# Strassen's seven products for both projections of a hybrid decoder layer

## The reference, cut to what matters

```python
h = rms_norm(x, norm_in)                      # x: 2048 x 1024
proj = h @ w_in                               # 1024 x 6400
cb, cc, cu, gate_c, q, k, v, gate_a = split(proj)   # k, v: 128 columns, the others 1024
conv_y = cb * short_conv(cc * cu, conv_w)     # causal, width 3
conv_y = rms_norm(conv_y, norm_conv_out) * silu(gate_c)
attn_y = sliding_window_attention(q, k, v, sinks)   # window 128, 16 heads, 2 kv heads
attn_y = rms_norm(attn_y, norm_attn_out) * silu(gate_a)
x = x + concat([conv_y, attn_y]) @ w_out      # 2048 x 1024
return rms_norm(x, norm_final)
```

## Time and profile before

| | |
|---|---|
| median of 3 runs | 1689.29 us (1688.45 to 1691.91) |
| span of the profiled execution | 1689.7 us |
| TensorE busy | 1638.5 us (97%) |
| VectorE busy | 1038.0 us (61%) |
| ScalarE busy | 560.3 us (33%) |
| GpSimd busy | 267.0 us (16%) |
| mean granted TensorE clock | 0.989 of full speed |

### The profile page before, as it was taken

How to read it: one execution, slowest core, us unless ns; L and a number is a source line. 1 busy time by engine, 2 the same in 40 slices (tenths; PEclk the granted TensorE clock), 3 DMA queues, 4 the chain that set the end, 5 groups by cost and what they waited for, 6 DMA issues and landing times.

```text
span 1689.7 us, 23074 instructions
## 1 busy us (share of the span) xinstructions
PE 1638.5 (97%) x7824; PEld 1370.7 (81%) x7824; DVE 1038.0 (61%) x2262; ACT 560.3 (33%) x1275; POOL 267.0 (16%) x229
## 2 busy tenths in 40 slices
PE   5999999999999998999999999999999899999996
PEld 4888888888888886788888888888888688888885
DVE  6376767667576758567667676766667643333332
ACT  6333433343333354333333333333333421111110
POOL 1021212122121302112122121312122000000000
PEclk9999999999999999999999999999999899999998
DMA  4112021121202152211121212112021532222220
GB/s 172 54 38 74 31 81 53 47 75 35 78 31 68 43 194 69 81 51 63 43 68 37 74 31 82 50 50 74 31 94 63 199 138 100 99 99 97 98 77 27
DMA packets 61774, 125.42 MB, mean 74 GB/s; under 512 B 4640, under 2 KB 37408, under 8 KB 59680
## 3 DMA queue, kind: packets, MB, share of 16 engines
q1 hardware_dynamic: 59424, 116.44, 20.2%
q0 software_dynamic: 2304, 8.39, 1.2%
HBM read 99.64 MB, written 25.17 MB: 74 GB/s over the span
## 4 chain that ended last, share of the span: by engine, by line
PE 84%; DVE 8%; issue 3%; ACT 3%; DMA 1%; SPq 0%; DVEq 0%; POOL 0%; ACTq 0%; POOLq 0%
PE job_bank L1260 57%; PE job_bank L1427 8%; PE score_bank L1427 5%; PE turn_bank L1427 5%; PE score_bank L1350 3%; PE out_bank L1377 3%; PE out_bank L1427 2%; DVE probs L1036 1%; PE turn_bank L1363 1%; DVE w_lo L822 1%; DVE hT_lo L857 1%; DVE tanh_sb L1089 1%; DVE pT_lo L1042 1%; ACT pT_hi L701 1%; DVE attn_y L1055 1%
## 5 line engine op out<-in xcount | busy, mean ns | idle before, releaser
L1260 PE MATMUL job_bank<-hT_hi,w_hi 128*128 128x512 f32 x1600 | 635.4, 397 | 9.9 <-DVE conv_y L1081 4.5
L1260 PE MATMUL job_bank<-hT_lo,w_hi 128*128 128x512 f32 x1600 | 627.7, 392 | 0.0
L1260 PE MATMUL job_bank<-hT_hi,w_lo 128*128 128x512 f32 x1600 | 627.7, 392 | 0.0
L1260 PEld LDWEIGHTS job_bank<-hT_hi,w_hi 128*128 128x128 f32 x1600 | 302.9, 189 | 70.2 <-issue 6.0
L1260 PEld LDWEIGHTS job_bank<-hT_hi,w_lo 128*128 128x128 f32 x1600 | 302.6, 189 | 65.5
L1260 PEld LDWEIGHTS job_bank<-hT_lo,w_hi 128*128 128x128 f32 x1600 | 303.2, 190 | 58.5
L512 POOL TENSOR_TENSOR probs<-probs,smax 128x512 f32<-128x512 f32 x64 | 66.6, 1040 | 795.6 <-DVE smax L1028 795.6
L688 ACT ACTIVATE probs<-probs,smax 128x128 f32<-128x128 f32 x256 | 99.8, 391 | 253.4 <-DVE smax L1020 253.4
L822 DVE TENSOR_TENSOR w_lo<-w_raw,w_hi 128x1024 fp32r<-128x1024 f32 x100 | 122.4, 1224 | 87.1 <-ACT w_hi L558 84.3
L701 ACT ACTIVATE pT_hi<-probs 128x512 fp32r<-128x512 f32 x128 | 80.7, 633 | 258.7 <-DVE probs L1036 257.0
L558 ACT ACTIVATE w_hi<-w_raw 128x1024 fp32r<-128x1024 f32 x100 | 105.3, 1053 | 0.8
(11 more groups left out here) (187 smaller groups left out, 2237.5 us busy)
## 6 DMA issues: line engine op xcount, KB each, us to landing
w_raw<-w_in SPq DMA_DIRECT2D x100, 512.0 KB, 3.3
mixed<-gated SPq DMA_DIRECT2D x64, 256.0 KB, 2.3
mix_raw<-mixed SPq DMA_DIRECT2D x16, 1024.0 KB, 6.4
x_sb<-x SPq DMA_DIRECT2D x18, 512.0 KB, 4.5
wo_raw<-w_out SPq DMA_DIRECT2D x16, 512.0 KB, 4.6
z<-x SPq DMA_DIRECT2D x16, 512.0 KB, 3.3
out<-z POOLq DMA_DIRECT2D x16, 512.0 KB, 2.9
probs<-x SPq DMA_DIRECT2D x2, 512.0 KB, 10.9
```

The source lines that it names most:

```text
L1260: ins = nc.tensor.matmul(job_bank[bank][:], w[:, slot, kt, :], h[:, kt, cols], start=(kt == 0 and n == 0), stop=(kt == KT - 1 and n == 2))
```

## The change

Both projections are rewritten as one level of Strassen's scheme (seven products and 15 sums in place of eight products and 4 sums). A block `n` is a pair of column tiles (in the output projection a pair of token tiles) by a pair of 512-wide chunks by the two halves of the contraction. It takes seven products (`product`), each of 4 contraction tiles by 3 matmuls, so 84 matmuls where the old jobs took 96.

The narrow operand is called `w` and has seven forms: the quarters W11, W12, W22 and the sums WA, WB, WC, WD, which GpSimd forms anew for every block (`weight_sums`). Each form of 128x512 is then rounded by ScalarE (`round_w`) and its rest taken by VectorE (`w_rest`). The wide operand `f` has seven forms too (M11 to M4), 128x2048 each; four "generations" of it exist (tokens of half 0, tokens of half 1, and the two halves of `w_out`). VectorE forms four of them (`f_sum`) and the rests of all (`f_rest`); ScalarE rounds them. `w_lo` lies over `w_sum`, and `f_lo` over `f_raw`, so a form can be written only after the last product that used the old one.

The results build up in PSUM banks X, Y0 or Y1, and Z. Between products ScalarE copies X into Y (`seed_y`), Z into SBUF (`take_p5`) and Y into Z (`seed_z`), and VectorE adds (`c22`, `c12`).

An iteration of a half is now three blocks: A (q and C), B (u and B) and C (the two gates), with the attention units placed between products. Gates are no longer applied there: y and the gate go to DRAM apart (`y_dram`, `g_dram`), and in the output projection GpSimd multiplies them (`mix`), ScalarE squares y, GpSimd folds the squares from 1024 to 128 columns (`fold`), and TensorE sums them with `ones` (`sum_squares`). The output projection goes through `w_out` half by half: blocks k = 0 to 7 do the convolution branch and store `z_part`, k = 8 to 15 the attention branch and the final norm. One probability transpose now serves both keys blocks (`merge` on GpSimd).

The core of the diff (left out: loads and stores, the attention functions, which keep their arithmetic, and the semaphores' declarations):

```diff
-    def job(slot, bank, ch):
-        cols = slice(ch * CHUNK, (ch + 1) * CHUNK)
-        for kt in range(KT):
-            for n, (w, h) in enumerate(((w_hi, hT_hi), (w_hi, hT_lo), (w_lo, hT_hi))):
-                ins = nc.tensor.matmul(job_bank[bank][:], w[:, slot, kt, :], h[:, kt, cols],
-                                       start=(kt == 0 and n == 0), stop=(kt == KT - 1 and n == 2))
-        ins.then_inc(job_done, 1)
...
-        for n, (m, part) in enumerate(((mix_hi, 0), (mix_hi, 1), (mix_lo, 0))):
-            for h in range(NH):
-                ins = nc.tensor.matmul(mix_bank[p][s][h], m[:, p, kt, :],
-                                       wo_part(kt, part)[:, h * CHUNK:(h + 1) * CHUNK],
-                                       start=(kt % TILES == 0 and n == 0),
-                                       stop=(kt % TILES == TILES - 1 and n == 2))
...
-    def mix_rest(p, t):
-        dve.wait_ge(mix_hi_ready, t + 1)
-        nc.vector.tensor_tensor(mix_lo[:, p], mix_raw[:, p], mix_hi[:, p].bitcast(F32), ALU.subtract
-                                ).then_inc(mix_ready, 1)
-    def wo_rest(kt):
-        dve.wait_ge(wo_hi_ready, kt + 1)
-        nc.vector.tensor_tensor(wo_part(kt, 1), wo_raw[:, kt % WO_RAW, :], wo_part(kt, 0).bitcast(F32),
-                                ALU.subtract).then_inc(wo_ready, 1)
...
+W11, WA, WB, W12, WC, WD, W22 = range(PRODUCTS)
+M11, M5, M6, M21, M7, M22, M4 = range(PRODUCTS)
+HK = KT // 2
+HALF_BLOCKS = 1 + 3 * TILES
+OUT_PAIRS = TT // 2
+BLOCKS = HALVES * HALF_BLOCKS + 2 * OUT_PAIRS
+GEN_FIRST = [0, HALF_BLOCKS, 2 * HALF_BLOCKS, 2 * HALF_BLOCKS + OUT_PAIRS]
...
+        nl = GEN_FIRST[gen] - 1
+        slot = (M11, M5, M21, M22)[q]
+        sp.wait_ge(prod_done, PRODUCTS * nl + slot + 1)
...
+        sp.dma_start(f_raw[:, slot], source).then_inc(f_landed[q], 16)
...
+        k = n - HALVES * HALF_BLOCKS
+        for s in which:
+            if s == 0:
+                if k < 0:
...
+            elif s == 1:
...
+                pool.wait_ge(summed, 4 * n + 1)
+                slot, one, two = WB, w_sum[:, W11], w_sum[:, WA]
+            elif s == 2:
+                slot, one, two = WC, w_sum[:, W11], raw2[:, 0]
...
+                pool.wait_ge(summed, 4 * n + 2)
+                slot, one, two = WD, w_sum[:, W12], w_sum[:, WB]
+            if n > 0:
+                pool.wait_ge(prod_done, PRODUCTS * (n - 1) + slot + 1)
+            nc.gpsimd.tensor_tensor(w_sum[:, slot], one, two, ALU.add).then_inc(summed, 1)
...
+    def mix(k, *which):
+        n = out_block(0, 0) + k
+        for q in which if k < 2 * OUT_PAIRS else ():
+            s, half = (1, 1, 0, 0)[q], q % 2
+            pool.wait_ge(mix_landed[s], 32 * (k + 1))
+            if q == 0:
+                pool.wait_ge(summed, 4 * (n - 1) + 3)
+            elif q == 1:
+                pool.wait_ge(w_ready[W22], n)
+            else:
+                pool.wait_ge(prod_done, PRODUCTS * (n - 1) + (W11, W12)[half] + 1)
+            dest = (raw2[:, 0], raw2[:, 1], w_sum[:, W11], w_sum[:, W12])[q]
+            cols = slice(half * CHUNK, (half + 1) * CHUNK)
+            nc.gpsimd.tensor_tensor(dest.rearrange("p k c -> p (k c)"), yb[:, s, cols], gb[:, s, cols],
+                                    ALU.mult).then_inc(mixed, 1)
...
+    def fold(k, s):
+        if k >= 2 * OUT_PAIRS:
+            return
+        base = 3 * (2 * k + 1 - s)
+        pool.wait_ge(y_squared, 2 * k + 2 - s)
+        b = sq(k, s)
+        nc.gpsimd.tensor_tensor(b[:, 0:512], b[:, 0:512], b[:, 512:1024], ALU.add).then_inc(sq_folded, 1)
+        pool.wait_ge(sq_folded, base + 1)
+        nc.gpsimd.tensor_tensor(b[:, 0:256], b[:, 0:256], b[:, 256:512], ALU.add).then_inc(sq_folded, 1)
+        pool.wait_ge(sq_folded, base + 2)
+        if k > 0:
+            pool.wait_ge(ssq_done, k)
+        nc.gpsimd.tensor_tensor(sq_fold[:, s], b[:, 0:128], b[:, 128:256], ALU.add).then_inc(sq_folded, 1)
...
+    for k in range(2 * OUT_PAIRS):
+        n = out_block(0, 0) + k
+        if k == 0:
+            fold(0, 1)
+            fold(0, 0)
+        mix(k + 1, 0, 1, 2)
+        sums(n + 1, 0, 1)
+        fold(k + 1, 1)
+        mix(k + 1, 3)
+        sums(n + 1, 2)
+        fold(k + 1, 0)
+        sums(n + 1, 3)
+        if k > 0:
+            store_out(k - 1)
...
+    def copy_b12(gen):
+        nl = GEN_FIRST[gen] - 1
+        act.wait_ge(f_landed[1], 16 * gen)
+        act.wait_ge(prod_done, PRODUCTS * nl + M7 + 1)
+        nc.scalar.activation(f_raw[:, M7], f_raw[:, M5], ACT.Copy).then_inc(f_copied, 1)
+    def seed_y(n):
+        act.wait_ge(prod_done, PRODUCTS * n + 1)
+        if n >= 2:
+            act.wait_ge(y_free[n % 2], n // 2)
+        nc.scalar.activation(bank_y(n)[:], X[:], ACT.Copy).then_inc(y_seeded, 1)
+    def take_p5(n):
+        act.wait_ge(prod_done, PRODUCTS * n + 2)
+        if n > 0:
+            act.wait_ge(p5_used, n)
+        nc.scalar.activation(p5[:], Z[:], ACT.Copy).then_inc(p5_taken, 1)
+    def seed_z(n):
+        act.wait_ge(prod_done, PRODUCTS * n + 3)
+        act.wait_ge(p5_taken, n + 1)
+        nc.scalar.activation(Z[:], bank_y(n)[:], ACT.Copy).then_inc(z_seeded, 1)
...
+    def w_rest(n, *slots):
+        for i in slots if n < BLOCKS else ():
+            dve.wait_ge(w_rounded[i], n + 1)
+            if i in (W11, WA, WB, W12):
+                dve.wait_ge(summed, 4 * n + {W11: 3, WA: 2, WB: 4, W12: 4}[i])
+            source = raw2[:, 1] if i == W22 else w_sum[:, i]
+            nc.vector.tensor_tensor(w_lo[:, i], source, w_hi[:, i].bitcast(F32), ALU.subtract
+                                    ).then_inc(w_ready[i], 1)
...
+    def f_sum(gen, i):
...
+            else:
+                dve.wait_ge(f_copied, gen)
+                dve.wait_ge(f_landed[0], 16 * gen)
+                one, two = f_raw[:, M11], f_raw[:, M5]
+            ins = nc.vector.tensor_tensor(f_raw[:, M5], one, two, ALU.subtract)
...
+            ins = nc.vector.scalar_tensor_tensor(out=f_raw[:, M6], in0=f_raw[:, M5], scalar=-1.0,
+                                                 in1=f_raw[:, M22], op0=ALU.mult, op1=ALU.subtract)
...
+    def f_rest(gen, i):
+        count = {M11: 1, M5: 2, M6: 3, M21: 3, M7: 4, M22: 4, M4: 3}[i]
+        dve.wait_ge(f_summed, 4 * gen + count)
+        dve.wait_ge(f_rounded[i], f_count(gen, i))
+        nc.vector.tensor_tensor(f_lo[:, i], f_raw[:, i], f_hi[:, i].bitcast(F32), ALU.subtract
+                                ).then_inc(f_ready[i], 1)
+    def c22(n, dest):
+        dve.wait_ge(prod_done, PRODUCTS * n + 5)
+        dve.wait_ge(p5_taken, n + 1)
+        nc.vector.tensor_tensor(dest, bank_y(n)[:], p5[:], ALU.add).then_inc(c22_ready, 1)
+    def c12(n):
+        dve.wait_ge(prod_done, PRODUCTS * n + 6)
+        nc.vector.tensor_tensor(p5[:], Z[:], p5[:], ALU.add).then_inc(c12_ready, 1)
...
+    def final_norm(k):
+        if k < OUT_PAIRS:
+            return
+        m = k - OUT_PAIRS
+        dve.wait_ge(z_squared, 2 * m + 2)
+        nc.vector.tensor_scalar(z_stat[:, :, 1:2], z_stat[:, :, 0:1], 1.0 / D_MODEL, EPS,
+                                ALU.mult, ALU.add).then_inc(z_var, 1)
+        dve.wait_ge(z_rooted, m + 1)
+        newton(*(z_stat[:, :, j:j + 1] for j in (3, 2, 1)))
+        if m == 0:
+            dve.wait_ge(gain_landed, 32)
+        for s in range(2):
+            nc.vector.scalar_tensor_tensor(out=zb[k % 2][:, s], in0=zb[k % 2][:, s], scalar=z_stat[:, s, 3:4],
+                                           in1=gain_final, op0=ALU.mult, op1=ALU.mult).then_inc(fin_ready, 1)
...
+        w_rest(n, W22)
...
+        else:
+            final_norm(k - 1)
+            w_rest(n + 1, WA)
+            add_z(k, 0)
+            c22(n, c2[:])
+        w_rest(n + 1, W11)
+        c12(n)
+        add_z(k, 2)
+        w_rest(n + 1, WB, W12)
+        add_z(k, 1)
+        add_z(k, 3)
+        w_rest(n + 1, WC, WD)
+        rms_y(k + 1)
...
+    def product(n, i):
+        gen = sum(n >= first for first in GEN_FIRST) - 1
+        pe.wait_ge(w_ready[i], n + 1)
...
+                pe.wait_ge(f_ready[i], f_count(gen, i))
+        if i == 0:
+            if n > 0:
+                pe.wait_ge(x_free, n)
+            bank, first = X, True
+        elif i == 1:
+            if n > 0:
+                pe.wait_ge(c12_ready, n)
+            bank, first = Z, True
+        elif i == 2:
+            pe.wait_ge(y_seeded, n + 1)
+            bank, first = bank_y(n), False
+        elif i == 3:
+            pe.wait_ge(y_seeded, n + 1)
+            bank, first = X, False
+        elif i == 4:
+            pe.wait_ge(z_seeded, n + 1)
+            bank, first = bank_y(n), False
+        elif i == 5:
+            pe.wait_ge(z_seeded, n + 1)
+            bank, first = Z, False
+        else:
+            pe.wait_ge(c22_ready, n + 1)
+            bank, first = bank_y(n), False
+        for kt in range(HK):
+            for j, (w, f) in enumerate(((w_hi, f_hi), (w_hi, f_lo), (w_lo, f_hi))):
```

(27 more changed lines are left out.)

2682 lines of the change are left out of this document (1580 added, 1102 removed).

## The result

The changed kernel takes 1778.63 us in the median of four runs (1773.05 to 1779.26), the kernel before 1689.44 (1688.45 to 1691.91, four runs): a ratio of 1.051, 95% interval 1.050 to 1.053. It is about 5% slower. I had forecast 1713, on the right side, but the time lies above my range of 1620 to 1760.

The account below looks back on a forecast made before the run. In the iterations, 1205 of 1689.7 us, the number of TensorE matmuls was taken as the bound. Head 79, iterations 1126, first iterations 5, change of halves 51 and output 452 summed to 1713 us, range 1620 to 1760.

Parts of the forecast that it names:

- The iterations: Sixteen iterations of the input projection: 70.4 us each, 1126 in all, against 1205 before.
- the list: Walk through one iteration's instructions in order: TensorE loses 2.1 us in block A, 0.6 in B, 0.9 in C.
- One sign of it: Sign of the forecast: GpSimd's sums with a mean of 1.5 us or more, where 1.27 is the minimum.
- Another: Sign of the forecast in the head: first product at 42 us.
- the head: Start of the kernel: last x tile turned at 42 us, then a first block of 37; 79 in place of 58.6.
- The first iteration: First iteration of each half: turns of x and of v in it, 5 us more for both together.
- the change of halves: Between the two halves of the input projection: new wide forms made on VectorE, 51 us, as much as before.
- The output term: Whole output projection: 58 + 46 + 7 x 22.5 + 7 x 25.5 + a tail of 12 = 452 us, against 375.2.
- k = 0: First output block: VectorE's chain of 25.2 us, first product at 13, GpSimd's work in the way; 58 us.
- The ring: Output blocks: GpSimd 13.9, VectorE 6.7, cut-ins 1.9; 22.5 us for k = 1 to 7, 25.5 from k = 9.
- The clock, my third rival: Output blocks: seventh product at half clock after TensorE's wait, 2.2 us more each, 31 in all, so 1744; chance 0.18.
- the lists keep up: Rival: GpSimd's instructions fit VectorE's gaps, 1 us lost per iteration, output blocks 20.2, total 1597 us; chance 0.20.

Follow-up runs that it names:

- The seventh experiment: Changed kernel, first iteration only: VectorE scales the last four x tiles in a row, TensorE turns them after products 2, 3, 3 and 4; 1771.1 us.
- the first experiment: Changed kernel with the next block's sum of squares moved behind the seventh product in TensorE's output list; 1756.5 us, ratio 1.040.
- The sixth experiment: Changed kernel, output block k = 0 only: first sum of squares moved behind the sixth product, the second behind the seventh; 1773.3 us, ratio 1.050.
- the second experiment: Changed kernel with 9 or 18 unused filler matmuls on TensorE ahead of the sum of squares in output blocks; 1761.3 us, ratio 1.044.
- the eleventh experiment: Kernel of the fifth experiment with one GpSimd fold per tile in place of three, squares of three quarters of the channels left out; 1706.9 us, ratio 1.009.
- the fourth experiment: Changed kernel with GpSimd's weight sums in the input projection replaced by one-operand multiplications by 1.0; 1776.1 us, ratio 1.052.
- the fifth experiment: Changed kernel with folds, sums of squares and root moved in the output blocks to where nothing waits for them; 1740.1 us, ratio 1.029.

## Why the prediction was wrong

**The iterations were right in sum.** All but the first and the fifth of a half take 68.3 to 70.6 us, 70.3 in most, forecast 70.4. The places differ from the list: in the six iterations from 172 to 594 us TensorE waits, counting waits above 0.25 us, 1.6 us per iteration before turning (for GpSimd's normalised probabilities) and 0.8 in four of the six before a weighing. I had 2.1 and 0.9 before two weighings and 0.6 before a turning. So that the sum came out to 0.1 is partly luck. One sign of it was wrong: GpSimd's 264 sums take 1.41 in the mean (1.29 in the median), not 1.5 or more. It is VectorE that mostly loses, its rests taking up to 1.78. Another was off by 3: the first product started at 39.0 us and not at 42, and the first block then took 42 and not 37, so the head was right in sum only.

**The first iteration was mis-sized by 16 us.** I gave 5 us for the first ones of both halves. Half 0's alone has 91.0: TensorE waits 8.6 and 3.5 for the last four tiles of x, whose squares end at 88.5 since the last of them lands by then, and two of which VectorE scales only behind WA's rest, for which it waits 9.1 itself. The seventh experiment gave 4 of it back in its profiled execution, and 7.6 in the median, by order alone. The fifth iterations, at 74.1 and 73.0, I had not set apart; with the same code they take 70.7 and 71.0 in the first experiment's kernel, and what makes them long stays open. The head and the change of halves were right to 2 and 3 us.

**The output term is the step that failed (452 forecast, 493.7 measured), and within it k = 0**, 81.6 for 58: "GpSimd has 8 gate products, 7 sums and 4 folds in the way" was said, but I costed them beside VectorE's passes and not ahead of TensorE's sums of squares, on which products 5 and 7 stand: 9.3 and 14.6 us. The sixth experiment returned 5 to 9 of the 24. The first product, 18.5 after the last scores and forecast at 13, is another 5.5: y and gate have landed by 1290.9, 7 us after the last scores, but W11's rest has to wait until GpSimd has done three gate products and three sums (to 1300.5), and then takes 1.67. Rows of GpSimd and VectorE ahead of the first sum of squares show what the lists cost each other here:

```profile
1290.85 4.57 POOL L654 TENSOR_TENSOR raw<-yb,gb 128x512 f32<-128x512 f32 x2 [13.54 <-DMA gb<-g_dram]
1320.14 2.52 POOL L664 TENSOR_TENSOR sq<-sq 128x512 f32<-128x512 f32 x1 [11.71 <-ACT sq L1028]
1321.43 3.38 DVE L1362 TENSOR_TENSOR f_raw<-f_raw 128x2048 f32<-128x2048 f32 x1
1331.48 2.38 POOL L670 TENSOR_TENSOR sq_fold<-sq 128x128 f32<-128x128 f32 x1
```

VectorE's passes of 128x2048 take 2.29 us and GpSimd's instructions 1.26, 0.72 and 0.45 (512, 256 and 128 wide) when nothing meets them; here single ones take up to 3.38 and 2.38 to 2.66. The six folds ahead of the first sum of squares take 11 us where the shortest of their kinds add up to 4.9, and they start late besides, since ScalarE's squares stand behind its roundings of the wide forms (GpSimd waits 11.7 and 2.4 us for them). The second sum of squares waits for almost the whole of a ring turn's list: GpSimd's second gate product for it may start only after W22's rest, at 1344.4, its last fold ends 15 us later, and TensorE stands before this sum from 1345 on. The rest, spread over slow products and waits of 1.4 to 2.2, I can't split further.

**The ring was right once its rival is taken out.** I forecast 22.5 and 25.5; the first and the second experiment measure 22.6 and 25.6 to 25.9. For k = 1 to 7 the terms hold too: in the first experiment's kernel GpSimd's list takes 14.1 us without its delays (forecast 13.9), VectorE's 6.3 with the hand-overs (6.7), and what the two engines cost each other on this path is 2.2 (1.9). The clock, my third rival (0.18), came true beside the forecast and not in its place: behind the waits of 2.2 and 4.4 us the seventh product ran for the most part or wholly at half clock, and it lies in the ring. I priced it at 31 us; the two kernels got 15 to 16 back, since the other path is only 0.9 us shorter in k = 1 to 7. The fault was to treat forecast and rival as alternatives: my own forecast had TensorE idle ahead of the seventh product, and the earlier trace rows said what follows.

**Of the others**, "the lists keep up" is refuted as a state of this kernel, but the eleventh experiment shows what it would have taken: 5 us less on GpSimd per block. The mutual exclusion that the Trainium skill describes (SBUF — State Buffer, Who interferes with whom: a VectorE instruction with two SBUF inputs contends with a GpSimd one that reads SBUF) is what the rests show beside GpSimd's sums of two operands, 1.70 to 1.78 us. For GpSimd instructions that read one operand the fourth experiment differs from it, and the measurement decides: of eight rests five were not delayed, and three by 0.4 us where 1.4 us of GpSimd's instruction were left. In the output ring the exclusion is 2.2 of the 22.6 us. It grew in the fifth experiment, by 1.7 us per block on VectorE and 1.6 on GpSimd, once the engines were freed of the ring; there GpSimd's list without its 3.0 us of stretching would by my sum be shorter than TensorE's 19.5.

## What to carry to other kernels

Before work is traded from the bound engine to idle ones, draw the ring: what one block's first instruction on each engine waits for, back to the same instruction of the block before. If the ring is longer than the block, matmuls saved give nothing, and the shortest remedy is to take out of it what nobody in it needs (the sum of squares here: 38 us). And if a forecast has TensorE wait some us in one piece, its next product has to be priced at half clock in the same sum, up to the length of the second path (here 5.3 us for 2.85 after 4.4 us, and 4.1 to 4.4 in most blocks after 2.2). Where a stage starts anew, as k = 0 does, an instruction that waits for the end of a long list is charged the whole list, with what the engines cost each other in it. A change in two halves is worth running as two: here one half won 31 us up to the last scores, and the other lost 118.

## What the runs showed of the hardware

A GpSimd instruction of 128x512 that reads one operand (a multiplication by a constant) took 1.49 us where a sum of two took 1.29. Behind waits of 2.2 us twelve matmuls took 4.1 to 4.4 us at granted clocks of 0.61 to 0.66 in four blocks (k = 2 to 5) and 2.85 at 1.00 in one (k = 6); behind 4.4 us they took 5.3 at 0.50; in the second experiment's kernel they took 4.4 at 0.61 behind 1.5 to 1.6 us (three of the blocks k = 9 to 14). Where the waits were 0.7 to 1.4 us (the first and second experiment, k = 2 to 5) the clock stayed at 1.00. A rest of 128x512 on VectorE that starts in a GpSimd sum of two operands with 1.1 to 1.2 us of it left took 1.70 to 1.78 us for 0.69, and a GpSimd fold of 128x128 beside a pass of 128x2048 2.38 for 0.45. The instructions of four output blocks took 10% (GpSimd) and 14% (VectorE) longer when the ring that made the engines wait for each other was gone.
